# The heads of a second attention in pairs, their scores one pair ahead in alternating PSUM banks

## The chip, the core and the metric

The kernel runs on one core of one Trainium2 chip. The metric is the device time of one execution in microseconds, and the number compared is the median of several runs.

## What is computed

Two blocks follow each other on 256 tokens of width 1024, all in fp32. The first block (a stick-breaking attention, a recurrence, a feed-forward part) isn't touched. The second has two layers, and the change lies in each layer's attention:

```python
def global_attention(q, k, v):          # heads 0 to 7: 8 query heads, 2 key heads, 64 wide
    sc = einsum('bqkgd,bskd->bkgqs', qblk, k) * scale
    p = softmax(sc, axis=-1)
    return einsum('bkgqs,bskd->bqkgd', p, v)

def window_sink_attention(q, k, v, sink, slopes):   # heads 8 to 15, as many keys
    sc = einsum('bqkgd,bskd->bkgqs', qblk, kb) * scale - slope * dist   # NEG_INF outside the window
    m = maximum(sc.max(-1), sink)
    p = exp(sc - m); p = p / (p.sum(-1) + exp(sink - m))
    return einsum('bkgqs,bskd->bqkgd', p, vb)

for l in range(2):
    qa, ka, va, qb, kb, vb = split(h @ w_in[l])      # qa, ka: RMS norm and rotation
    oa, ob = rms_norm(global_attention(qa, ka, va)), rms_norm(window_sink_attention(qb, kb, vb, ...))
    h = layer_norm(ALPHA * h + concat([oa, ob]) @ w_o[l])
    h = layer_norm(ALPHA * h + peer_ffn(h))
```

## The kernel before

It is written engine by engine: `tensor`, `scalar`, `vector`, `gpsimd` and `sync` each issue their own instructions in a fixed order by hand, and semaphores tie them (`s.up(key, step)` marks a step, `w.wait_ge(*s.to(step))` waits for it). So each engine is a queue in program order: what stands behind a waiting instruction waits too. `emptied(b)` on TensorE waits until PSUM bank `b` has been read by whoever reads it last (`free[b]`). There are eight banks of 128x512 fp32.

Weights come as units of 128x1024. SyncE loads them into three raw slots, ScalarE rounds them into a high part (`hi`, L1123, two halves of 128x512 a unit), GpSimd or VectorE subtracts to get the low part (`lo`, GpSimd's at L2341). High and low parts have six halves each, so three units are ready ahead. A product takes three matmuls (high by high, high by low, low by high) in place of an fp32 one.

The attention of a layer works on 16 heads of 64 numbers. Heads 0 to 7 are the first group (global attention), 8 to 15 the second (window and sink). `QT` holds the transposed queries and keys: tiles 0 to 3 the queries of the first group, 4 its keys, 5 to 8 and 9 the same of the second. Each tile has the heads of key head 0 on partitions 0 to 63 and those of key head 1 on 64 to 127 (`PAR`), so head 0 and head 4 share tile 0 and lie on different partitions. For a head:

- TensorE `at_scores`: two fp32 matmuls of contraction 64, 256 columns each, into bank `h % 2`. An fp32 matmul stands as two records in the trace.
- VectorE `at_scores`: row maximum (L2062) and its product with the scale (L2069) for the first group; for the second, distance bias (L1621, writes `WS`), maximum, maximum with the sink, scale (L1618). It gives `nmx`.
- ScalarE `at_scores`: two exponentials with sums (L1135) into `PX[h % 3]`.
- TensorE `at_turn`: four 128x128 transposes (L445) into bank `2 + h % 2`; VectorE (heads 0 to 7, L2117) or ScalarE (8 to 15, L1514) copies the bank to `PT`.
- TensorE `at_pv`: four fp32 matmuls of 64 columns into banks 6 and 7 (first group) or 4 and 5 (second).

The loop runs over single heads, 18 steps; in step `h` TensorE issues the scores of head `h`, transposes head `h-1`, issues five filler matmuls (`warm`, bf16, into a score bank; nothing reads the result), and makes the value product of head `h-2`:

```python
        for h in range(18):
            if h < 16: at_scores(h)
            if h < 2: project(2, 2 + h, 4)
            if 5 <= h < 10: turn_tile((9, 5, 6, 7, 8)[h - 5], 2 + h % 2, ("qb", l))
            if h in (15, 16): turn_out("oa", [h - 15], OA)
            if 1 <= h <= 16:
                at_turn(h - 1)
                if h > 2: warm((h - 1) % 2, 5)
            if h == 17: out_product(0)
            if h >= 2: at_pv(h - 2)
```

`project(2, g, 4)` are the last two quarters of the input projection. `turn_tile` transposes the second group's query and key tiles, one a step from step 5 on, copied by VectorE (L2019). Inside the same loop VectorE scales the residual `H` and adds its bias (`gain_step`, L1959, four of 128x1024, steps 4 to 7), and normalises the first group's output: `over` (reciprocal of the sums), `values` (L2089), `head_mean`, `head_root`, `head_norm` (L2107), for which GpSimd squares (L2402) and ScalarE takes a root, with a table load before and after. `turned`/`turn_out` transpose the normalised output for the output product: TensorE, then ScalarE (high part), then VectorE (low part, L1621). `out_product(n)` takes the units of `w_o`, 12 matmuls of 512 columns each; 0 to 3 need the first group alone, 4 to 7 the second. After the loop come turns 2 and 3 of the first group, products 1 to 3, the second group's turns (its normalisation runs on VectorE and ScalarE meanwhile), products 4 to 7 and a layer norm.

## Time and profile before

| | us |
|---|---|
| median of 3 runs | 2468.97 |
| lowest and highest run | 2467.76, 2470.97 |
| the profiled execution's own time | 2468.69 |
| its span, first to last instruction | 2466.9 |
| TensorE, VectorE, ScalarE, GpSimd busy in it | 2406.5, 1682.1, 1261.8, 541.0 |
| head loop of layer 0, first score matmul to first output product | 58.43 |
| the same of layer 1 | 58.43 |

The profile is of one execution. Busy time of an engine is the time in which at least one of its instructions runs; matmuls overlap in it, so starts, not durations, tell how long TensorE takes for a group. The granted clock is the share of full speed at which TensorE's clock was let through.

The columns of the rows further down: in a timeline, start in us from the span's start, duration in us, engine, line, operation, written tile <- read tiles, partitions x elements, how many instructions are merged (x), and in brackets the idle time before and what ended it. In the windows view, the stretch, its length, then busy us and instructions of TensorE's matmuls (PE), its weight loads (PEld), VectorE (DVE), ScalarE (ACT) and GpSimd (POOL), then the granted clock, the DMA engines' busy share and GB/s. `arena`, `pb` and `cst` are the SBUF area of all working tiles, the PSUM banks and the constants.

### The profile page before, as it was taken

The numbers are of one execution on the slowest core, as the hardware profiler recorded it, in microseconds if no ns is written. First come the engines' busy times: TensorE is split into PE (matmuls) and PEld (weight loads), VectorE is DVE, ScalarE is ACT, GpSimd is POOL, SyncE is SP. The second block draws the span as 40 slices with busy tenths as digits, with TensorE's granted clock in tenths as the row PEclk, the third lists the DMA queues.
The fourth block names the chain that finished last, engine by engine and source line by source line (L and its number), as shares of the span: only waits on it lengthen the run. The fifth ranks groups of instructions, "written<-read, shape, count | busy, mean of one in ns | idle before, by whom it ended". The sixth has DMA issues, their size and how long they took to land.

```text
span 2466.9 us, 42599 instructions
## 1 busy us (share of the span) xinstructions
PE 2406.5 (98%) x16775; PEld 2183.0 (88%) x16775; DVE 1682.1 (68%) x3026; ACT 1261.8 (51%) x2689; POOL 541.0 (22%) x423
## 2 busy tenths in 40 slices
PE   7999999999999999999999999999999999999997
PEld 6888989998789999999888888789999999888886
DVE  4737345446669767887777556659776888777556
ACT  6542335445555544445555555545455455555554
POOL 3640224546178300000000002358500000000000
PEclk9999999999999999999999999999999999999999
DMA  5320145564145666666777665235666666787664
GB/s 179 121 87 17 36 153 169 188 188 143 49 156 171 186 181 194 195 195 193 241 245 224 195 211 151 90 113 168 183 187 185 195 193 193 227 247 237 195 199 145
DMA packets 148069, 421.00 MB, mean 171 GB/s; under 512 B 15904, under 2 KB 49056, under 8 KB 147488
## 3 DMA queue, kind: packets, MB, share of 16 engines
q1 hardware_dynamic: 144080, 405.34, 53.2%
q0 software_dynamic: 2192, 8.99, 1.0%
q10 hardware_dynamic: 1600, 3.96, 0.5%
q8 instruction: 134, 2.20, 0.4%
q14 instruction: 63, 0.52, 0.1%
HBM read 400.40 MB, written 17.83 MB: 170 GB/s over the span
## 4 chain that ended last, share of the span: by engine, by line
PE 92%; DVE 4%; ACT 2%; DMA 1%; issue 0%; POOL 0%; ACTq 0%; DVEq 0%
PE pb L436 91%; PE pb L445 1%; ACT arena L1135 1%; DVE arena L1618 1%; DVE arena L1621 0%; ACT L1135 0%; DVE arena L1767 0%; DMA raw<-in_vT 0%; DMA H<-in_x 0%; ACT hi L1123 0%; DVE H L1618 0%; DVE sm L1932 0%; DVE arena L2062 0%; DVE arena L1791 0%; DMA raw<-in_w_out 0%
## 5 line engine op out<-in xcount | busy, mean ns | idle before, releaser
L1123 ACT CAST hi<-raw 128x512 fp32r<-128x512 f32 x1402 | 819.2, 620 | 376.4 <-PE pb L436 192.5
L436 PE MATMUL pb<-HTh,hi 128*128 128x256 f32 (+1 forms) x2968 | 858.9, 289 | 2.6 <-POOL lo L2341 1.9
L436 PE MATMUL pb<-HTh,lo 128*128 128x256 f32 (+1 forms) x2968 | 842.2, 284 | 0.0
L436 PE MATMUL pb<-HTl,hi 128*128 128x256 f32 (+1 forms) x2968 | 842.2, 284 | 0.0
L2341 POOL TENSOR_TENSOR lo<-raw,hi 128x512 fp32r<-128x512 f32 x383 | 520.2, 1382 | 564.1 <-ACT hi L1123 564.1
L1628 DVE TENSOR_TENSOR lo<-raw,hi 128x1024 fp32r<-128x1024 f32 x464 | 565.3, 1218 | 85.7 <-ACT hi L1123 85.5
L436 PEld LDWEIGHTS pb<-HTh,hi 128*128 128x128 f32 x2968 | 569.7, 192 | 7.2 <-issue 2.7
L436 PEld LDWEIGHTS pb<-HTl,hi 128*128 128x128 f32 x2968 | 570.1, 192 | 0.9
L436 PEld LDWEIGHTS pb<-HTh,lo 128*128 128x128 f32 x2968 | 569.6, 192 | 0.0
L436 PE MATMUL pb<-hi,WH 128*128 128x512 f32 x1112 | 433.6, 390 | 4.3 <-DVE WL L2305 4.3
L436 PE MATMUL pb<-lo,WH 128*128 128x512 f32 x1112 | 433.2, 390 | 0.0
L436 PE MATMUL pb<-hi,WL 128*128 128x512 f32 x1112 | 433.0, 389 | 0.0
L1135 ACT ACTIVATE arena<-pb 128x256 f32<-128x256 f32 (+1 forms) x301 | 114.8, 382 | 472.8 <-PE pb L436 469.8
L2348 POOL DMA_DIRECT2D arena<-in_ln_g x4 | 2.3, 563 | 1273.9 <-PE pb L436 1273.9
L2305 DVE TENSOR_TENSOR WL<-arena,WH 128x256 fp32r<-128x256 f32 x256 | 109.9, 429 | 230.0 <-ACT WH L1587 229.0
L436 PEld LDWEIGHTS pb<-hi,WH 128*128 128x128 f32 x1112 | 208.9, 188 | 48.2 <-ACT arena L1135 3.1
L436 PEld LDWEIGHTS pb<-hi,WL 128*128 128x128 f32 x1112 | 208.8, 188 | 43.2
L436 PEld LDWEIGHTS pb<-lo,WH 128*128 128x128 f32 x1112 | 208.9, 188 | 42.5
L436 PE MATMUL pb<-arena 128*128 128x128 f32 (+13 forms) x1808 | 208.9, 278 | 4.1 <-DVE arena L1791 1.5
L436 PEld LDWEIGHTS pb<-arena 128*128 128x128 f32 (+6 forms) x1808 | 180.1, 174 | 22.1 <-issue 6.2
L1635 DVE TENSOR_TENSOR lo<-raw,hi 128x512 fp32r<-128x512 f32 x91 | 90.3, 994 | 38.7 <-ACT hi L1123 36.6
L1587 ACT CAST WH<-arena 128x256 fp32r<-128x256 f32 x256 | 102.5, 401 | 1.8 <-PE pb L436 1.8
(196 smaller groups left out, 2166.0 us busy)
## 6 DMA issues: line engine op xcount, KB each, us to landing
raw<-in_uT SPq DMA_DIRECT2D x256, 512.0 KB, 3.6
raw<-in_vT SPq DMA_DIRECT2D x256, 512.0 KB, 4.2
raw<-in_w_ffn_in SPq DMA_DIRECT2D x44, 512.0 KB, 4.0
raw<-in_wq SPq DMA_DIRECT2D x32, 512.0 KB, 3.6
wk<-kept SPq DMA_DIRECT2D x128, 128.0 KB, 3.8
raw<-in_w_in SPq DMA_DIRECT2D x24, 512.0 KB, 3.8
raw<-in_w_ffn_out SPq DMA_DIRECT2D x22, 512.0 KB, 4.4
raw<-in_w_gate SPq DMA_DIRECT2D x16, 512.0 KB, 3.3
```

What stands on the lines that cost most here:

```text
L436: return e.matmul(o, l, r, start=start, stop=stop)
L445: return e.transpose(o, i, m.C("ident")[0:n, 0:n])
L1123: e.copy(u.hi[k], u.half[k]).then_inc(*s.up("hi", ("hi", g)))
L1135: return e.activation(o, a, f, **kw)
L1587: e.copy(m.AC[j % 2][0], m.AW[:, j, :]).then_inc(*s.up("w_hi", ("w_hi", l, j)))
L1618: return e.tensor_scalar(o, a, s1, None, op0) if op1 is None else e.tensor_scalar(o, a, s1, s2, op0, op1)
L1628: x = tt(u.lo2, u.raw, u.hi2.bitcast(F32), S)
L1635: tt(u.lo[k], u.half[k], u.hi[k].bitcast(F32), S).then_inc(*s.up("lo_dve", ("lo", g)))
L2305: tt(m.AC[j % 2][1], m.AW[:, j, :], m.AC[j % 2][0].bitcast(F32), S).then_inc(*s.up("w_low", ("w_lo", l, j)))
L2341: tt(u.lo[k], u.half[k], u.hi[k].bitcast(F32), S).then_inc(*s.up("lo_pool", ("lo", g)))
L2348: e.dma_start(bc[:, 0:1024], g.partition_broadcast(128)).then_inc(*s.up(f"bc{n}", by=16))
```

## The change

On TensorE the heads are taken in eight pairs in the order 0 4, 1 5, 2 6, 3 7, 8 12, 9 13, 10 14, 11 15: one head on partitions 0 to 63 and one on 64 to 127. The matmuls of a pair's scores alternate between the two heads and between two banks, and the banks of one pair differ from those of the next (`SCORES`). The scores of pair p+1 are issued before the value products of pair p-2 and behind the transposes of pair p-1. The fillers are six before the scores of four pairs and six before the last transposes. The five tiles of the second group are transposed together in pair 2, through banks 4 and 5, and ScalarE copies them instead of VectorE. `PT` has four buffers. VectorE's residual steps go to pairs 0 (two), 2 and 4. VectorE's bias step waits for the exponential three heads before it. The first group's normalisation moves by some heads, its four turns stand behind transposes 15 and value product 14 and use banks 0 and 1, and the first output product comes behind them and behind the last value product. In the code `n` is a head's place in the new order.

```diff
+HEADS = [0, 4, 1, 5, 2, 6, 3, 7, 8, 12, 9, 13, 10, 14, 11, 15]
+TILES = (9, 5, 6, 7, 8)
+SCORES = ((0, 1), (6, 7), (0, 1), (4, 5), (0, 1), (4, 5), (0, 1), (6, 7))
...
-        self.PT = [ar(13824 + i * 512, 512) for i in range(3)]
+        self.PT = [ar(13824 + i * 512, 512) for i in range(3)] + [ar(0, 512)]
...
-FOUR, OA, OBT = (0, 1, 2, 3), (3, 2), (2, 3, 4, 5)
+FOUR, OA, OBT = (0, 1, 2, 3), (0, 1), (2, 3, 4, 5)
...
+        def at_scores(p):
+            pair = list(zip(SCORES[p], HEADS[2 * p:2 * p + 2]))
+            for b, h in pair:
+                f = 5 * (h // 8)
+                emptied(b)
+                w.wait_ge(*s.to("qt", l, f + h % 4))
+                w.wait_ge(*s.to("qt", l, f + 4))
             for t in range(2):
-                x = mm(PB[b][:, t * 256:(t + 1) * 256], m.QT[r, f + j, t * 128:(t + 1) * 128], m.QT[r, f + 4, :], True, True)
+                for b, h in pair:
+                    r, f = PAR[h % 8 // 4], 5 * (h // 8)
+                    x = mm(PB[b][:, t * 256:(t + 1) * 256], m.QT[r, f + h % 4, t * 128:(t + 1) * 128], m.QT[r, f + 4, :], True, True)
+                    if t:
+                        x.then_inc(*s.up("score_ps", ("score_ps", l, h)))
+                        free[b] = [("nmx" if h > 7 else "px", l, h)]
...
-        for h in range(18):
...
+        at_scores(0)
+        at_scores(1)
+        project(2, 2, 4)
+        project(2, 3, 4)
+        for p in range(1, 8):
+            at_turn(2 * p - 2)
+            at_turn(2 * p - 1)
+            if p < 7 and p != 2:
+                if p > 2:
+                    warm(SCORES[p + 1][0], 6)
+                at_scores(p + 1)
+            if p > 1:
+                at_pv(2 * p - 4)
+                at_pv(2 * p - 3)
+            if p == 2:
+                for k, f in enumerate(TILES):
+                    turn_tile(f, 4 + k % 2, ("qb", l))
+                at_scores(3)
+        warm(0, 6)
+        at_turn(14)
+        at_pv(12)
+        at_pv(13)
+        at_turn(15)
+        turn_out("oa", (0, 1), OA)
+        at_pv(14)
         turn_out("oa", (2, 3), OA)
+        at_pv(15)
+        out_product(0)
...
+        def weights(n):
+            w.wait_ge(*s.to("pt_ps", l, HEADS[n]))
+            w.wait_ge(*s.to("pv_ps", l, HEADS[n - 4]))
+            e.copy(m.PT[n % 4], PB[2 + n % 2][:, :]).then_inc(*s.up("soft", ("pt", l, HEADS[n])))
+
+        for p in range(8):
+            if p == 7:
                 w.wait_ge(*s.to("o_ms", l, 0))
                 fn(m.s16[:, :, 0:8], m.v16[:, :, 0:8], ACT.Sqrt).then_inc(*s.up("roots", ("o_root", l, 0)))
+            at_scores(2 * p)
+            if p == 7:
+                weights(12)
+            at_scores(2 * p + 1)
+            if p == 0:
+                take("win", l, 2, 2)
+                take("win", l, 2, 3)
+            elif p == 1:
+                second_group()
+            elif p == 2:
+                for k, f in enumerate(TILES):
+                    w.wait_ge(*s.to("qt_ps", l, f))
+                    e.copy(m.QT[:, f, :], PB[4 + k % 2][:, 0:256]).then_inc(*s.up("qkv2", ("qt", l, f)))
+            elif p == 3:
+                split_high(units.i + 3)
+            elif p == 7:
                 w.wait_ge(*s.to("sinks", l))
...
+            if 3 < p < 7:
+                weights(2 * p - 2)
+                weights(2 * p - 1)
+        weights(14)
+        turned(("oa", l), (0, 1), OA, f"gn{l}")
         turned(("oa", l), (2, 3), OA, f"gn{l}")
...
             if g:
+                w.wait_ge(*s.to("px", l, HEADS[n - 3]))
                 stt(m.WS[i], C("negd"), 8.0 * 2.0 ** -(hh + 1), src, M, A).then_inc(*up("scores"))
...
+        for p in range(8):
+            at_scores(2 * p)
+            at_scores(2 * p + 1)
+            for k in {0: (0, 1), 2: (2,), 4: (3,)}.get(p, ()):
+                gain_step(k, ("in", l), m.BC2 if l else m.bc, 2 * l)
+            if 1 <= p <= 3:
+                weights(2 * p - 2)
+                weights(2 * p - 1)
+            elif p == 5:
                 over(0)
                 values(0, 0)
                 values(0, 1)
+            elif p == 6:
                 head_mean(0, 0)
                 head_mean(0, 1)
+            elif p == 7:
+                weights(13)
                 own()
                 sink = m.bcs[:, o + 128:o + 136].unsqueeze(2).to_broadcast([128, 8, 2])
                 tt(m.snk[:, 8:16, :], m.nmx[:, 8:16, :], sink, A).then_inc(*up("scores", ("sinks", l)))
+        head_root(0)
+        head_norm(0, 0)
+        head_norm(0, 1)
+        weights(15)
+        turned(("oa", l), (0, 1, 2, 3), OA, f"gn{l}")
         over(1)
```

ScalarE's and VectorE's `at_scores` take `n` too, with `h = HEADS[n]` and the bank from `SCORES`; VectorE has a `weights(n)` of its own.

## Rows read from the trace of the kernel before

**Rows 1.** The page: busy time, share of the span and instructions of each engine.

```profile
PE 2406.5 (98%) x16775; PEld 2183.0 (88%) x16775; DVE 1682.1 (68%) x3026; ACT 1261.8 (51%) x2689; POOL 541.0 (22%) x423
```

**Rows 2.** Windows of both head loops and one spell: busy times, granted clock, DMA.

```profile
610.84:669.27 58.43, 54.27 (x356) 44.26 (x357) 40.44 (x78) 31.46 (x92) 14.20 (x13) 1.00 0.20 64
...
1550.84:1609.27 58.43, 54.27 (x352) 44.22 (x352) 40.43 (x78) 31.46 (x92) 14.23 (x13) 0.99 0.20 64
1608.30:1611.70 3.40, 3.40 (x15) 3.05 (x14) 0.91 (x3) 0.78 (x2) 0.00 (x0) 0.50 0.00 0
```

**Rows 3.** Timeline of TensorE in both loops: start us, duration, instructions.

```profile
610.84 1.13 PE L436 MATMUL pb<-arena 64*128 64x256 f32 x4 [0.52 <-DVE arena L2019]
611.89 0.51 PE L436 MATMUL pb<-hi,HTh 128*128 128x512 f32 x1
...
618.79 0.60 PE L445 MATMUL pb<-cst,arena 128*128 128x128 f32 x4
...
649.41 0.66 PE L445 MATMUL pb<-cst,arena 128*128 128x128 f32 x4
649.90 0.71 PE L436 MATMUL pb<-cst 128*128 128x256 bf16 x5
650.45 2.06 PE L436 MATMUL pb<-arena 128*128 128x64 f32 x12
652.51 0.66 PE L445 MATMUL pb<-cst,arena 128*128 128x128 f32 x4
...
666.53 0.44 PE L445 MATMUL pb<-cst,arena 128*128 128x128 f32 x2 [1.30 <-ACT arena L1514]
...
669.27 0.48 PE L436 MATMUL pb<-hi,HTh 128*128 128x512 f32 x1
...
672.11 1.00 PE L436 MATMUL pb<-arena 128*128 128x64 f32 x8
672.95 0.61 PE L445 MATMUL pb<-cst,arena 128*128 128x128 f32 x4
673.31 0.47 PE L436 MATMUL pb<-hi,HTh 128*128 128x512 f32 x1
...
681.60 1.03 PE L445 MATMUL pb<-cst,arena 128*128 128x128 f32 x8
...
1613.73 1.00 PE L436 MATMUL pb<-arena 128*128 128x64 f32 x8
```

**Rows 4.** Groups of TensorE, layer 0's loop: transposes; busy, mean, idle before, releasers.

```profile
L445 PE MATMUL pb<-cst,arena 128*128 128x128 f32 x82 | 12.8, 283 | 4.2 <-ACT arena L1135 2.4 <-ACT arena L1514 1.3 <-DVE HTl L1621 0.5
```

**Rows 5.** Timeline of TensorE, first attention: one pair of heads on different partitions.

```profile
111.49 0.70 PE L436 MATMUL pb<-arena 64*128 64x256 f32 x4 [0.47 <-ACT arena L1235]
```

**Rows 6.** Timeline of VectorE in layer 0's loop.

```profile
629.34 0.69 DVE L2062 TENSOR_REDUCE arena<-pb 128x2 f32<-128x512 f32 x1 [0.41 <-PE pb L436]
...
631.07 1.21 DVE L1959 TENSOR_TENSOR H<-H,arena 128x1024 f32<-128x1024 f32 x1
...
655.85 0.69 DVE L1621 SCALAR_TENSOR_TENSOR arena<-cst,pb 128x512 f32<-128x512 f32 x1
...
657.49 0.17 DVE L1618 TENSOR_SCALAR arena<-arena 128x2 f32<-128x2 f32 x1
```

**Rows 7.** Timeline of ScalarE in layer 0's loop.

```profile
640.93 0.51 ACT L1135 ACTIVATE arena<-arena 128x256 f32<-128x256 f32 x1 [2.97 <-DVE arena L1618]
...
641.84 0.19 ACT L1135 ACTIVATION_READ_ACCUMULATOR arena<-arena 128x1 f32 x1
...
655.39 0.56 ACT L1514 COPY arena<-pb 128x512 f32<-128x512 f32 x1
655.97 1.28 ACT L1135 ACT_TABLE_LOAD   x1
...
658.79 0.51 ACT L1135 ACTIVATE arena<-arena 128x256 f32<-128x256 f32 x1
```

**Rows 8.** Timeline of GpSimd: low parts of four halves of w_o.

```profile
675.84 5.95 POOL L2341 TENSOR_TENSOR lo<-raw,hi 128x512 fp32r<-128x512 f32 x4 [22.66 <-ACT hi L1123]
```

More of the change, by code:

```diff
@@ L949, in tensor, with at_turn @@
         turn_tile(4, 2, ("ka", l))
[L952 to L964 removed]
+        def at_scores(p):
[5 more added lines that the diff above has]
+                w.wait_ge(*s.to("qt", l, f + 4))
+            for t in range(2):
+                for b, h in pair:
[4 more added lines that the diff above has]
+                        free[b] = [("nmx" if h > 7 else "px", l, h)]
+        def at_turn(n):
+            h, i, b = HEADS[n], n % 3, 2 + n % 2
             emptied(b)
@@ L971, in at_turn, with at_pv @@
             free[b] = [("pt", l, h)]
-        def at_pv(h):
-            i, g, hh = h % 3, h // 8, h % 8
+        def at_pv(n):
+            h, i = HEADS[n], n % 4
+            g, hh = h // 8, h % 8
             vo = 768 * g + 640 + 64 * (hh // 4)
@@ L1484, in second_group, with at_scores @@
                 e.copy(m.PJ[:, t, 1408:1536], PB[4 + t][:, 384:512]).then_inc(*s.up("qkv2", ("pj", l, 2, t), *([("vb", l)] if t else [])))
-        def at_scores(h):
-            g, hh, b, i = h // 8, h % 8, h % 2, h % 3
+        def at_scores(n):
+            h = HEADS[n]
+            g, b, i = h // 8, SCORES[n // 2][n % 2], n % 3
             src = m.WS[i] if g else PB[b][:, :]
@@ L1492, in at_scores @@
                 w.wait_ge(*s.to("nmx", l, h))
[L1493 to L1494 removed]
+                if n > 2:
+                    w.wait_ge(*s.to("pt_ps", l, HEADS[n - 3]))
                 x = fn(m.PX[i][:, t * 256:(t + 1) * 256], sv[:, t, :], ACT.Exp, bias=m.nmx[:, h, t:t + 1],
@@ L1497, in at_scores @@
                 x.then_inc(*s.up("soft", *([("px", l, h)] if t else [])))
-        for h in range(18):
-            if h == 2:
-                second_group()
-            elif h == 9:
-                split_high(units.i + 3)
-            elif h == 13:
+        def weights(n):
[4 more added lines that the diff above has]
+            if p == 7:
                 w.wait_ge(*s.to("o_ms", l, 0))
                 fn(m.s16[:, :, 0:8], m.v16[:, :, 0:8], ACT.Sqrt).then_inc(*s.up("roots", ("o_root", l, 0)))
-            if h < 16:
-                at_scores(h)
-            if h < 2:
-                take("win", l, 2, 2 + h)
-            if 9 <= h <= 16:
-                w.wait_ge(*s.to("pt_ps", l, h - 1))
-                w.wait_ge(*s.to("pv_ps", l, h - 4))
-                e.copy(m.PT[(h - 1) % 3], PB[2 + (h - 1) % 2][:, :]).then_inc(*s.up("soft", ("pt", l, h - 1)))
-            if h in (15, 16):
-                turned(("oa", l), [h - 15], OA, f"gn{l}")
-            if h == 15:
+            at_scores(2 * p)
[14 more added lines that the diff above has]
+            elif p == 7:
                 w.wait_ge(*s.to("sinks", l))
                 fn(m.snk[:, 8:16, :], m.snk[:, 8:16, :], ACT.Exp).then_inc(*s.up("soft", ("snk", l)))
+            if 3 < p < 7:
[3 more added lines that the diff above has]
+        turned(("oa", l), (0, 1), OA, f"gn{l}")
         turned(("oa", l), (2, 3), OA, f"gn{l}")
@@ L2051, in vector, with at_scores @@
         ts(m.sk8, m.bcs[:, o + 128:o + 136], 8.0, None, M).then_inc(*up("scores"))
-        def at_scores(h):
-            g, hh, b, i = h // 8, h % 8, h % 2, h % 3
+        def at_scores(n):
+            h = HEADS[n]
+            g, hh, b, i = h // 8, h % 8, SCORES[n // 2][n % 2], n % 3
             src = PB[b][:, :]
@@ L2108, in head_norm, with weights @@
             x.then_inc(*up("heads", ("os", l, g, t)))
-        for h in range(18):
-            if h < 16:
-                at_scores(h)
-            if 5 <= h < 10:
-                turn_tile((9, 5, 6, 7, 8)[h - 5], 2 + h % 2)
-            if 1 <= h <= 8:
-                w.wait_ge(*s.to("pt_ps", l, h - 1))
-                e.tensor_copy(m.PT[(h - 1) % 3], PB[2 + (h - 1) % 2][:, :]).then_inc(*up("tiles", ("pt", l, h - 1)))
-            if 4 <= h <= 7:
-                gain_step(h - 4, ("in", l), m.BC2 if l else m.bc, 2 * l)
-            if h == 10:
+        def weights(n):
+            w.wait_ge(*s.to("pt_ps", l, HEADS[n]))
+            if n > 3:
+                w.wait_ge(*s.to("pv_ps", l, HEADS[n - 4]))
+            e.tensor_copy(m.PT[n % 4], PB[2 + n % 2][:, :]).then_inc(*up("tiles", ("pt", l, HEADS[n])))
+        for p in range(8):
[7 more added lines that the diff above has]
+            elif p == 5:
                 over(0)
                 values(0, 0)
-            elif h == 11:
                 values(0, 1)
-            elif h == 12:
+            elif p == 6:
                 head_mean(0, 0)
                 head_mean(0, 1)
-            elif h == 13:
-                head_root(0)
-                head_norm(0, 0)
-            elif h == 14:
-                head_norm(0, 1)
-            elif h == 15:
+            elif p == 7:
+                weights(13)
                 own()
```

31 lines of the change are left out of this document (removed).

## The prediction

> **What bounds the kernel now.** I read the page first. TensorE is busy for 98% of the span [rows 1], and there is no core but this one, so a change in one stage counts only as far as TensorE gets through that stage sooner. Next the windows view: each layer's head loop, from the first score matmul to the first output product, is 58.43 us long with TensorE busy for 54.27 of them, the same in both layers, at the full granted clock but for a spell at its lower level (0.50) at 1608.30 in layer 1 [rows 2]. Then TensorE's own timeline [rows 3]. The reader should see that a steady head is a string of work with no gap: transposes from 649.41, five filler matmuls from 649.90, then from 650.45 in one line the value products of an older head and the scores of the next, and the next transposes at 652.51; 3.10 us a head. What the 16 heads wait for in all is one row: 4.2 us before the transposes, for ScalarE's exponentials and copies and one VectorE result [rows 4]. So the loop is bound by TensorE's instruction string and only in places by the softmax chain. VectorE and ScalarE were read last, for how long that chain is [rows 6, 7].
>
> **What the scores cost, and what pairing saves.** The scores of one head (two fp32 matmuls, four records, contraction over 64 rows) take 1.05 us from their start to the next instruction (610.84 to 611.89) [rows 3]; 16 heads, 16.8 us. The change interleaves a head on partitions 0 to 63 with one on 64 to 127, in two banks. The loop of before has no such pair, but the first attention has: four records of 64x256 in 0.70 us at 111.49 [rows 5], where four in a string take 1.13 [rows 3]; the two heads' records start together. I take a pair at 1.05, eight pairs 8.4: **saved 8.4 us**. Bounds: nothing if these pairs do not overlap, 8.4 if they do; the row is of the same shape, so the upper end.
>
> The Trainium skill, "TensorEngine Tiling (Array Packing)", sections "Tiling Modes" and "PSUM Bottleneck", speaks partly against it: changing the tiling mode drains the engine, and after the tiling the emptying of PSUM may become the bottleneck. The drain is inside the measured 1.05 and now comes 8 times instead of 16; the second is what the walk below looks for.
>
> **Fillers.** Before, 14 heads carry five bf16 fillers, 70 in all, 0.55 us for five (649.90 to 650.45), 0.11 each [rows 3]. After, five blocks of six, 30. **Saved 40 x 0.11 = 4.4 us.** They are busy time that waits may take back, so the waits have to be laid out.
>
> **Waits.** Saved: all of the old 4.2 us [rows 4]. New ones come from laying out the eight pairs in program order. TensorE: a pair of transposes 0.93 (0.49 for the first head, 649.41 to 649.90, 0.44 for the second), fillers 0.66, a score pair 1.05 and 0.1 lead, two heads of value products 1.8 (0.84 for one, 672.11 to 672.95, and its lead) [rows 3]: 4.5 us a pair against 6.2 before. VectorE: a first-group head 0.9 (reduction 0.69 and a small multiply with its wait), a second-group head 1.84 (655.85 to the end of 657.49, and the wait for itself), a scale or bias of the residual 1.2 [rows 6]; emptying a bank is taken at the reduction's 0.69. ScalarE: an exponential pair of halves 1.0, a bank copy 0.56, a table load 1.28 [rows 7].
>
> - *Start.* Two score pairs, then both projections: 610.84 + 2.1 + 5.8 = 618.75, where the first transposes stood before (618.79) [rows 3]. The 16 heads' scores are a pair further by then, and VectorE has done two scale steps in time that it idled.
> - *Pair 2.* Five q/k tile turns now stand together in two banks, copied by ScalarE behind exponentials 4 and 5. Value products 0 and 1 end at 623.55; ScalarE gets to the tiles at 624.15, the last copy ends at 626.25, and the next scores want its bank: they start at 626.3. Of 2.75 us, 1.2 are turns: **wait 1.5**. Late behind it: nothing but TensorE's own string.
> - *Pairs 3 to 5.* Scores of pair 4 start at 629.05, of 5 at 633.6, of 6 at 638.2: TensorE's 4.5 a pair. The chain from a score start is 1.2 (scores done), 3.65 (two heads on VectorE), 1.0 (exponential), 0.5 (copy) = 6.4 us, and the transposes that need it stand 7.4 us behind that start: 1 us of slack, no wait.
> - *Pair 6 to 7.* VectorE waits for value product 7 (641.15) before it scales the first group's output (0.69 twice), and the reductions of pair 6, whose scores are done at 639.35, are queued behind it. Their results come at 644.5 and 646.35; ScalarE's exponential of head 13 ends at 647.4, and its copy of transpose 10, queued behind that, at 647.95. Transpose 12 writes the bank which that copy empties; TensorE has been free since 645.6: **wait 2.35**.
> - *Pair 7.* ScalarE changes its table for the root and back (2.8 us, as 655.97 to 658.79 before [rows 7]) until 651.25, exponential 14 ends at 652.25, copy 12 at 652.8; transpose 14 waits for its bank from 651.3: **wait 1.5**.
> - *End.* The last turns of the first group cost about 0.4; the output products start at 658.6, value product 15 and all turns behind them already. Before, they start at 669.27 but the product after the first only at 673.31, since the last value product and two turns stand between [rows 3]. Level with 673.31 is 658.6 + 2.75 = 661.35: 11.96 us sooner.
>
> **Sum.** By parts, 8.4 + 4.4 + 4.2 - (1.5 + 2.35 + 1.5 + 0.4 = 5.75) = 11.3 us a layer; by the layout 11.96. I take 11.7. Parts moved at no cost: PT's fourth buffer; VectorE's added wait for the exponential three heads back (done by then); the residual's four steps, 4.8 us of VectorE, of which two lie before 618.75 and two behind reductions that are early. If that cover goes, a step is 1.2. The five tile copies are 5 x 0.3 more for ScalarE, in the 1.5. No DMA is moved past another queue; SyncE and GpSimd issue as before.
>
> **Does it come through?** The second group's chain begins when value product 15 ends. Before, it fits behind three products: its turns start at 681.60, right behind the third [rows 3]. After, it has four. GpSimd makes low parts at 5.95 / 4 = 1.49 a half, 2.98 a unit [rows 8], against 2.84 of a product (669.27 to 672.11); three units are ready, so five later ones could lag by 0.7 us. That stays in the range.
>
> **Clock.** After the same waits, 1.30 us at 666.53 among them, only layer 1 got its spell at 0.50, and there value product 15 starts 62.89 us behind the first score instead of 61.27: a spell costs 1.62 us [rows 2, 3, 5]. The new waits are longer and the fillers fewer, so I expect a spell in each layer, one more than now.
>
> 2 x 11.7 - 1.6 = 21.8 us. The profiled execution took 2468.69 us, span 2466.9; span after 2445.1. The median of the runs is 0.28 above that execution: **2468.97 - 21.8 = 2447.2 us**. Its own range: no spells and no new waits but the two at the pairs 6 and 7, 2442; 3 us more of waits a layer, 2453.
>
> **Rivals.**
> 1. *The softmax chain paces the second group.* The 1 us of slack is thin, and VectorE's other work sits in the same queue. If all four pairs 4 to 7 take 6.4 instead of 4.5, that is 7.6 us less the 3.85 already counted: gain 8.0 a layer, 2454.6. For it: VectorE's load a pair is 3.7 plus extras. Against: the extras stand in two pairs alone. Chance 0.12.
> 2. *The paired scores run in a string.* 8.4 us come back, about 3 of them inside the new waits: gain 6.3 a layer, 2458. Against it stands 111.49 [rows 5]. Chance 0.03.
> 3. *It is paid back later*: the second group's chain or the low parts hold TensorE at the output products until what was won is gone: no change, 2467. What they can hold by the rows above is under 1 us. Chance 0.04.
> 4. *Slower: TensorE's clock.* With 40 fillers gone and micro-waits between groups the granted clock could stay at 0.50 (1.2 GHz). At 1.62 us a spell it takes seven spells a layer to eat 11.7 us; the whole loop at the lower level would double 41.5 us of work: 2 x (41.5 - 11.7) = 60 slower, 2529. Against: in both layers a loop with 4.2 us of waits got at most one spell. Chance 0.03.
>
> On rival 4 the Trainium skill, "TensorE: Matmul & The Clock Gate", section "A second HAM failure mode: psum-queue depth-cycling", says that short idles between groups of matmuls that cycle through PSUM banks can make the clock swing between its levels again and again. By that rule this loop, with alternating banks, would lose time as rival 4 does; by the rows of before, whose loop also cycles banks, it does not.
>
> **Chances.** The forecast 0.78. A difference under 0.2% (4.9 us) is about what a measurement of this kernel cannot tell from none. Faster: forecast, rivals 1 and 2, 0.93; within 0.2%: rival 3 and the near side of 4, 0.04; slower 0.03. Range for 8 in 10: 2439 (no waits beyond 3 us a layer, no spells) to 2457 (rival 1 with 1 us more of waits a layer).
>
> **What would show it.** TensorE's score rows come as eight records in about 1.13 us, 8 times a layer; 30 fillers a layer; the head loop's window from the first score to the first output product about 47.8 us instead of 58.43. Waits before transposes 12 and 14 on ScalarE's copies, and before the fourth score pair on ScalarE's last tile copy. The second group's turns follow the fourth product. One spell at 0.50 near the loop's end in each layer. The prediction is wrong if transposes wait in every pair, if the score pairs take 2 us, or if the stretch between the loop and the layer norm has grown.

## The result and the profile after

| | before | after |
|---|---|---|
| median of 7 runs, us | 2470.97 | 2448.77 |
| lowest and highest run | 2467.76, 2471.92 | 2440.83, 2456.60 |
| the profiled execution's own time, its span | 2468.69, 2466.9 | 2454.43, 2452.6 |
| granted clock, mean of the span | 0.993 | 0.988 |

The ratio of the times is 0.9912, 95% interval 0.9898 to 0.9927: faster by 0.9%, 22.2 us between the medians where 21.8 were predicted. The runs of after spread over 15.8 us, those of before over 4.2.

The page of after, busy times, to be held against [rows 1]: TensorE has 13.7 us less, 80 matmuls fewer, which are the fillers.

```profile
PE 2392.8 (98%) x16695; PEld 2173.9 (89%) x16695; DVE 1676.7 (68%) x3016; ACT 1264.9 (52%) x2699; POOL 541.3 (22%) x423
```

The windows of both head loops of after (first score to first output product) and of a spell in each, as in [rows 2]:

```profile
609.58:662.27 52.69, 48.76 (x329) 42.15 (x329) 39.38 (x74) 33.77 (x99) 14.43 (x13) 0.87 0.20 71
647.20:660.80 13.60, 13.43 (x65) 13.12 (x65) 7.30 (x16) 7.53 (x18) 0.00 (x0) 0.50 0.01 1
1544.94:1597.57 52.63, 48.71 (x328) 42.10 (x329) 39.39 (x74) 33.77 (x99) 14.45 (x13) 0.87 0.20 71
1582.40:1596.10 13.70, 13.37 (x65) 13.06 (x65) 7.32 (x17) 7.69 (x18) 0.00 (x0) 0.50 0.00 0
```

Layer 0's loop is 5.7 us shorter than before, not the 10.6 that were forecast (58.43 to about 47.8), and the granted clock says why: it is 0.87 in the mean, because each loop holds a spell of 13.7 us at 0.50, TensorE's lower level (1.2 GHz). TensorE was busy for 13.4 of these 13.7 us, so this is work done slowly. In layer 1 the gain is 6.7: the loop of before is 59.35 there, not 58.43, because its first output product starts only at 1610.19, behind the end of the window in [rows 2]:

```profile
1610.19 0.77 PE L436 MATMUL pb<-hi,HTh 128*128 128x512 f32 x1
```

A second profile of the same kernel (the run `after_again` below) happens to have no spell in layer 0's loop and 3.4 us of one in layer 1's:

```profile
611.15:659.42 48.27, 42.98 (x328) 35.96 (x329) 39.51 (x75) 33.58 (x99) 14.42 (x13) 1.00 0.24 77
1541.78:1590.09 48.31, 44.36 (x328) 37.66 (x329) 39.56 (x75) 33.59 (x99) 14.46 (x13) 0.96 0.23 77
```

That is the loop which the prediction laid out: 48.27 us long (47.8 predicted). TensorE's timeline of it, from the second group's tiles in pair 2 on; the rows answer to [rows 3]. The last row is ScalarE's, the copy that empties the bank of transpose 10:

```profile
624.51 0.71 PE L448 MATMUL pb<-cst,arena 128*128 128x128 f32 x4 [0.55 <-ACT arena L1541]
625.41 0.44 PE L448 MATMUL pb<-cst,arena 128*128 128x128 f32 x2 [0.19 <-ACT arena L1541]
626.30 1.13 PE L439 MATMUL pb<-arena 64*128 64x256 f32 x8 [0.46 <-ACT arena L1541]
627.37 1.09 PE L448 MATMUL pb<-cst,arena 128*128 128x128 f32 x8
...
629.05 3.06 PE L439 MATMUL pb<-arena 64*128 64x256 f32 x24
631.95 1.04 PE L448 MATMUL pb<-cst,arena 128*128 128x128 f32 x8
...
637.35 1.14 PE L448 MATMUL pb<-cst,arena 128*128 128x128 f32 x8 [0.71 <-ACT arena L1523]
...
642.27 1.14 PE L448 MATMUL pb<-cst,arena 128*128 128x128 f32 x8
...
648.92 1.14 PE L448 MATMUL pb<-cst,arena 128*128 128x128 f32 x8 [1.86 <-ACT arena L1523]
...
653.81 0.66 PE L448 MATMUL pb<-cst,arena 128*128 128x128 f32 x4 [1.35 <-ACT arena L1523]
...
641.66 0.56 ACT L1523 COPY arena<-pb 128x512 f32<-128x512 f32 x1
```

Read it in pairs of heads. The scores of a pair are eight records in 1.13 us at 626.30, and the next thing starts 1.07 later. Three waits of the prediction's layout are there: at the tiles 0.55 + 0.19 + 0.46, before transpose 12 (648.92) 1.86, before transpose 14 (653.81) 1.35. Two are there that it didn't have: 0.71 before transpose 8 (637.35), and a small one before transpose 10 (642.27), which carries no mark of its own. That transpose stands 4.92 behind transpose 8, where a pair without a wait takes 4.5, and it starts 0.05 behind the end of ScalarE's copy (641.66 + 0.56); so some 0.4 went there.

To compare loops whatever stands at their end, I take the "level": from the first score to the product behind the first output product, 62.47 us before in layer 0 (673.31 in [rows 3] less 610.84). It is 51.11 in `after_again`: **11.36 us a layer at the full clock**. With the 13.7 us spell it is 55.54: the spell costs 4.43. Layer 1 of before has a spell of its own in [rows 2], and its level is 64.09.

### The profile page after: what moved, and what is told of

The parts are those of the page before. It is cut to its first block and busy times, and to the rows that moved or that the text cites. A ratio compares the mean times of both kernels' runs of the same rounds, so it can differ in the third digit from the quotient of the medians.

```text
span 2452.6 us, 42445 instructions
## 1 busy us (share of the span) xinstructions
PE 2392.8 (98%) x16695; PEld 2173.9 (89%) x16695; DVE 1676.7 (68%) x3016; ACT 1264.9 (52%) x2699; POOL 541.3 (22%) x423
## 5 line engine op out<-in xcount | busy, mean ns | idle before, releaser
L439 PE MATMUL pb<-arena 128*128 128x128 f32 (+13 forms) x1808 | 196.2, 282 | 5.0 <-DVE arena L1823 1.5
L439 PEld LDWEIGHTS pb<-arena 128*128 128x128 f32 (+6 forms) x1808 | 174.1, 178 | 23.8 <-issue 9.8
```

The costliest lines, as they stand in the source:

```text
L439: return e.matmul(o, l, r, start=start, stop=stop)
```

## The experiments

Each time is a median; "before" is the old kernel on the same chip, and the interval is that of the ratio. The level and the spells at 0.50 inside the loops are those of each profiled execution.

| kernel | us | before | ratio, 95% | level, layers 0 and 1 | spells, layers 0 and 1 |
|---|---|---|---|---|---|
| after_again | 2449.03 | 2469.21 | 0.9905 to 0.9935 | 51.11, 51.16 | none, 3.4 |
| same_rows | 2457.63 | 2469.21 | 0.9940 to 0.9964 | 61.69, 55.84 | 3.4 + 13.7, none |
| fill_waits | 2445.55 | 2469.21 | 0.9892 to 0.9921 | 51.13, 51.39 | none |
| copies_first | 2441.79 | 2469.21 | 0.9869 to 0.9898 | 50.17, 50.19 | none |
| before_30_fill | 2481.14 | 2469.56 | 1.0025 to 1.0058 | 68.74, 69.31 | 27.3, 27.3 |
| residual_late | 2451.38 | 2469.56 | 0.9910 to 0.9937 | 52.85, 53.10 | 6.8, 6.8 |
| copies_fill | 2444.96 | 2469.56 | 0.9882 to 0.9911 | 50.17, 50.88 | none |
| root_late | 2445.12 | 2469.56 | 0.9875 to 0.9906 | 50.80, 50.77 | none |
| scores_behind | 2443.61 | 2468.02 | 0.9883 to 0.9913 | 50.29, 50.31 | none |
| no_fill | 2454.49 | 2468.02 | 0.9925 to 0.9952 | 55.81, 55.94 | 6.8 + 10.2, 10.2 + 6.8 |
| cast_late | 2441.77 | 2468.02 | 0.9879 to 0.9909 | 49.19, 50.92 | none, 6.8 |
| copies_first_2 | 2444.47 | 2468.02 | 0.9886 to 0.9916 | 50.18, 50.20 | none |

### after_again: the changed kernel once more

No edit. 

> The changed kernel once more, as the reference of the three below. Theory A (the gain is saved TensorE work, and spells at the lower clock level give some of it back, by chance more or less from run to run): the median lies between 2441 and 2457 again, runs spread by over 8 us, and a run's time rises as its mean granted clock falls. Theory B (the spread is noise of the measurement and has nothing to do with the clock): times and mean clock do not go together.

It gives 2449.03, and the loop without a spell, shown above. The runs spread over 10.2 us, and longer runs have the lower clock in the main: over the 7 runs of after and these 6, a straight line through time and clock gives 0.35 us for each us at 0.50. Theory A stands, though not run by run (2451.83 came at 0.988, 2453.98 at 0.990).

### same_rows: what the two halves of the array are worth

```diff
-HEADS = [0, 4, 1, 5, 2, 6, 3, 7, 8, 12, 9, 13, 10, 14, 11, 15]
+HEADS = [0, 1, 2, 3, 4, 5, 6, 7, 8, 9, 10, 11, 12, 13, 14, 15]
```

The order of the work stays, but both heads of a pair lie on the same partitions. 

> The pairs are 0 1, 2 3, 4 5 and so on, both heads of a pair on the same partitions, all else as in the changed kernel. Theory A (8.4 us a layer come from two heads' score matmuls running at once): a pair's eight records take 2.1 us instead of 1.14; TensorE's string is 8.4 us a layer longer, of which waits swallow up to 3: 11 to 17 us slower than the changed kernel, 2460 to 2466. Theory B (the gain comes from the fillers and the waits alone, the scores are hidden): within 3 us of the changed kernel.

TensorE's timeline of it: a pair alone, and a string of a pair and two value products (3.06 us at 629.05 above).

```profile
627.64 1.99 PE L439 MATMUL pb<-arena 64*128 64x256 f32 x8 [0.46 <-ACT arena L1541]
...
643.63 3.92 PE L439 MATMUL pb<-arena 64*128 64x256 f32 x24
```

A pair takes 1.99 in place of 1.13, 0.86 more, 6.9 a layer. The level of layer 1, which has no spell here, is 4.7 longer, because waits give back most of the rest: those before transposes 8 and 10 are gone (1.1), the one before transpose 12 is 1.32 instead of 1.86, the first one at the tiles 0.24 instead of 0.55. The medians differ by 8.6 us, under the 11 to 17 that I expected. So overlap is real, and it is the largest part of the gain, but only two thirds of it come through.

### before_30_fill: the fillers alone

The kernel before, with 30 fillers a layer instead of 70 and nothing else changed:

```diff
-                    warm((h - 1) % 2, 5)
+                    warm((h - 1) % 2, 3 if h in (15, 16) else 2)
```

> The kernel before with 30 fillers a layer in its head loop in place of 70 (two a head, three in two heads), all else as before. Theory A (the fillers are part of TensorE's string, 0.11 us each, where it has no wait): each loop is up to 4.4 us shorter at full clock, less what the waits of the second half take back; with one more short spell at the lower clock level: 3 to 8 us faster than the kernel before. Theory B (the loop of before is bound by the softmax chain, fillers only fill): no change within 2 us. Theory C (the fillers held the clock up): spells of several windows a layer, slower than before.

It is slower than before by 11.6 us: theory C. The windows view of layer 0's loop and of the spell in each layer:

```profile
610.44:675.15 64.71, 62.37 (x316) 49.79 (x317) 40.72 (x77) 31.43 (x92) 14.18 (x13) 0.79 0.16 58
645.90:673.20 27.30, 27.30 (x101) 21.52 (x99) 13.33 (x31) 12.50 (x35) 2.08 (x2) 0.50 0.03 10
...
1594.80:1622.10 27.30, 27.30 (x103) 21.78 (x100) 13.62 (x33) 11.59 (x33) 2.08 (x2) 0.50 0.05 19
```

With 40 matmuls fewer the loop is 6.28 us longer than [rows 2] (64.71 against 58.43), since 27.3 us of it ran at the lower level. TensorE's timeline on both sides of the fall:

```profile
644.78 0.63 PE L445 MATMUL pb<-cst,arena 128*128 128x128 f32 x4 [1.54 <-ACT arena L1135]
...
648.76 1.11 PE L445 MATMUL pb<-cst,arena 128*128 128x128 f32 x4
...
653.83 1.12 PE L445 MATMUL pb<-cst,arena 128*128 128x128 f32 x4
```

Up to 644.78 the edit does what was meant: that row stands 34.34 us behind the first score, where its counterpart in the kernel before (646.41, with a wait of 0.86) stands 35.57 behind it. By then 21 fillers are missing, 2.3 us, and 1.23 us have come through; longer waits took the rest back (2.14 us up to here instead of 1.10). The last of them has grown to 1.54 and the clock falls 1.1 us behind it; then a step of one head takes 5.07 (648.76 to 653.83) instead of 3.10. No gap in the loop is longer than that 1.54. What the removal would give behind that row at the full clock, no run shows.

### no_fill and fill_waits: fewer and more fillers in the changed kernel

`no_fill` takes out the 30 that are left, `fill_waits` adds 26 where TensorE waits anyway:

```diff
         for p in range(1, 8):
+            if p == 7:
+                warm(0, 16)
...
-        warm(0, 6)
+        warm(0, 16)
         at_turn(14)
```

> The changed kernel with none of its 30 fillers a layer. At full clock 3.3 us of string less a layer, of which waits take back what is in front of them. Theory A (what a filler buys is the granted clock: without them the loop runs at the lower level for much of its length, as the kernel before did for 27 us with 30 instead of 70): spells of 14 us or more in both loops, 0 to 12 us slower than the changed kernel. Theory B (fillers are only work): 3 to 6 us faster.

> The changed kernel with 16 more fillers before transpose 12 and 16 instead of 6 before transpose 14, where TensorE waits for 1.9 and (at full clock) 1.5 us. Theory A (the long spell at 0.50 near each loop's end comes of TensorE's idle time there and costs 4 to 5 us a layer): the spell goes, runs draw together, 6 to 9 us faster than the changed kernel, 2440 to 2443. Theory B (fillers are only work; the spell comes of something else, as the slow exchange of heads itself): no gain, same spells, 0 to 3 us slower.

`no_fill`: the two spells in layer 0's loop, windows view.

```profile
639.90:646.70 6.80, 6.80 (x34) 5.70 (x30) 3.51 (x8) 3.13 (x10) 0.85 (x1) 0.50 0.00 0
653.50:663.70 10.20, 9.16 (x45) 8.97 (x44) 5.46 (x12) 5.71 (x16) 0.00 (x0) 0.50 0.01 2
```

`fill_waits`: TensorE's timeline from transpose 12 on.

```profile
645.43 1.91 PE L439 MATMUL pb<-cst 128*128 128x256 bf16 x16
...
650.16 1.91 PE L439 MATMUL pb<-cst 128*128 128x256 bf16 x16
652.34 0.66 PE L448 MATMUL pb<-cst,arena 128*128 128x128 f32 x4 [0.27 <-ACT arena L1525]
```

Without fillers the wait before transpose 8 grows to 2.03, the loop holds 17.0 us at 0.50, and the time is 2454.49: 30 fillers (3.3 us) a layer less to do, and 5.5 us longer in all than `after_again`. That comparison is across two chips and the intervals overlap a little (up to 0.9935, from 0.9925); the three other kernels run beside `no_fill` on its chip are 10 to 13 us faster, with intervals apart. With 26 more layer 0's loop is as long as in `after_again` (48.29 against 48.27), as a filler in a wait costs nothing; layer 1's is 0.2 longer, for a longer wait at the tiles. Neither loop has a spell. The median, 2445.55, is 3.5 us under `after_again`, not the 6 to 9 of theory A, and the intervals overlap, so that the fillers keep the spells away is suggested and not shown; the highest of its 4 runs is 2447.52, of 6 runs of `after_again` 2453.98.

### copies_first: which wait holds transpose 12

ScalarE copies the transposed weights 10 and 11 ahead of exponentials 12 and 13, not behind them.

```diff
+            if p == 6:
+                weights(10)
+                weights(11)
             at_scores(2 * p)
...
-            if 3 < p < 7:
+            if 3 < p < 6:
                 weights(2 * p - 2)
```

> The changed kernel, but in pair 6 ScalarE copies transposes 10 and 11 before its exponentials 12 and 13, not behind them. Theory A (transpose 12 waits 1.9 us for a bank that a copy empties, and the copy waits in ScalarE's queue behind an exponential whose maximum is late on VectorE): transpose 12 starts with exponential 12, transpose 13 waits under 1 us, the loop is 1.0 to 1.3 us shorter a layer: 2 to 3 us faster at the same clock. Theory B (the late maximum itself holds TensorE): the wait moves whole to transpose 13 and nothing is gained.

> copies_first again, beside the three others. If its gain over the changed kernel was more than chance, the median is 2438 to 2445 and no loop has a spell longer than one of 3.4 us; else it falls among the changed kernel's 2441 to 2457.

TensorE's waits in the second half of its loop:

```profile
635.91 1.14 PE L448 MATMUL pb<-cst,arena 128*128 128x128 f32 x8 [0.71 <-ACT arena L1523]
647.01 0.66 PE L448 MATMUL pb<-cst,arena 128*128 128x128 f32 x4 [0.95 <-ACT arena L1154]
651.41 0.66 PE L448 MATMUL pb<-cst,arena 128*128 128x128 f32 x4 [1.36 <-ACT arena L1523]
```

Transpose 12 no longer waits; transpose 13 does, 0.95 for its own exponential. The loop gets 0.95 shorter, in both layers and in both profiles of this kernel: theory A. The first time the median was 7.2 us under `after_again` on the same chip, with intervals apart. 1.9 us of that are the waits; the rest may be spells that don't come (granted clocks 0.993 to 0.996, against 0.988 to 0.993). The second time, on another chip, it was 2444.47: inside the range expected, with no spell in a loop, but 23.6 us under the kernel before instead of 27.4, and its interval overlaps those of `after_again` and of after. The 0.95 a layer is shown, the 7 us is not.

`copies_fill` is this with 8 and 16 fillers ahead of transposes 12 and 14.

> ScalarE's copies of transposes 10 and 11 first, as in copies_first, and fillers in the waits that are left: 8 before transpose 12, 16 instead of 6 before transpose 14. Theory A (fillers in a wait cost nothing and keep the clock up): loops as long as those of copies_first at full clock, no spell in them, a median 0 to 3 us below that of copies_first, 2439 to 2442, and a spread under 5 us. Theory B (the fillers delay the transposes they stand before): 1 to 3 us slower than copies_first.

The loop is that of `copies_first` in layer 0 and 0.7 longer in layer 1, half of it in a wait of 0.92 instead of 0.58 at the tiles. 2444.96 where 2439 to 2442 were expected: nothing more is won by it.

### root_late: the table load and the root behind exponential 15

On top of `copies_fill` ScalarE takes the root after the last copy, and the four turns of the first group stand together behind value product 15. VectorE copies transpose 15 before it finishes the norm. The fillers differ too: 12 instead of 16 before transpose 14, and six new ones before the turns.

> As copies_fill, and ScalarE takes the first group's root, with its two table loads, behind exponentials 14 and 15 and copy 14 instead of ahead of them; the group's four turns stand behind value product 15 and use four banks. Theory A (the 2.8 us of table loads in front of exponential 14 are what holds transpose 14): its wait falls by 1 to 1.5 us, but the root and the norms come later and the first output product waits for them up to 2 us: loop 1 us shorter to 1 us longer. The second group's chain starts about 1.5 us sooner, which helps nothing while four products cover it. 2438 to 2443. Theory B (transpose 14 waits for VectorE's maximum): no difference there, and 1 to 2 us a layer slower at the end.

TensorE at transpose 14, and ScalarE's exponential 14:

```profile
653.23 1.47 PE L439 MATMUL pb<-cst 128*128 128x256 bf16 x12
654.76 0.66 PE L448 MATMUL pb<-cst,arena 128*128 128x128 f32 x4
...
653.14 0.51 ACT L1156 ACTIVATE arena<-arena 128x256 f32<-128x256 f32 x1 [2.19 <-DVE arena L1653]
```

No wait is marked before transpose 14, because the 12 fillers cover it. From the value products' end it takes 1.53 us to the transpose (653.23 to 654.76) instead of the 2.17 of `copies_fill`: the table loads held it for 0.6 us, not for 1 to 1.5, and behind them stands VectorE's maximum, for which ScalarE now waits (2.19). At the end the turns start only when VectorE's norm is done, the six fillers cover that, and 0.52 stands at the first output product (DVE's low part); the turns have lost their cover. The level is 0.63 longer than that of `copies_fill` in layer 0, the time the same (2445.12). The 1.35 us of transpose 14 can be moved in part, but aren't won this way.

### residual_late: VectorE's residual steps in pairs 3 to 6

```diff
-            for k in {0: (0, 1), 2: (2,), 4: (3,)}.get(p, ()):
+            for k in {3: (0,), 4: (1,), 5: (2,), 6: (3,)}.get(p, ()):
```

> The changed kernel with the residual's four steps on VectorE one each in pairs 3, 4, 5 and 6 instead of two in pair 0 and one each in 2 and 4. Theory A (VectorE's queue is what holds transposes 12 and 14, so a 1.2 us step ahead of them counts in full): the waits before transposes 12 or 14 grow by 1 to 2.4 us together, the loops get longer by as much: 2 to 5 us slower than the changed kernel. Theory B (VectorE has room in every pair): within 1 us.

2451.38. The waits grow in other places than theory A had them: before transpose 12 there are still 1.86 and 1.83, but before transpose 8 the wait is 0.92 instead of 0.71, and in layer 1 transpose 10 waits 0.49. Both loops have a spell of 6.8. How much of the 1.7 to 1.9 us of level belongs to the waits and how much to the clock, these runs don't separate, and the interval overlaps that of `after_again`.

### scores_behind: must the scores stand ahead of the value products?

```diff
-                at_scores(p + 1)
             if p > 1:
                 at_pv(2 * p - 4)
                 at_pv(2 * p - 3)
+            if p < 7 and p != 2:
+                at_scores(p + 1)
```

This starts a pair's scores two value products, some 1.8 us, later in TensorE's order. 

> The changed kernel, but a pair's scores are issued behind the two value products instead of ahead of them, 1.8 us later in TensorE's string; no instruction more or less. Theory A (scores issued early are what keeps the chain of scores, maximum, exponential and copy under TensorE's string, with about 1 us to spare in a pair): transposes wait about 1 us in each pair from 4 on and 1.8 more before 12: loops 3 to 6 us longer, 6 to 12 us slower in all than the changed kernel. Theory B (the place does not matter, TensorE's work decides): within 2 us.

I expected it to be slower. TensorE's timeline:

```profile
627.19 1.09 PE L448 MATMUL pb<-cst,arena 128*128 128x128 f32 x8
...
631.67 1.09 PE L448 MATMUL pb<-cst,arena 128*128 128x128 f32 x8
...
637.38 1.14 PE L448 MATMUL pb<-cst,arena 128*128 128x128 f32 x8 [1.17 <-ACT arena L1524]
...
642.31 1.14 PE L448 MATMUL pb<-cst,arena 128*128 128x128 f32 x8 [0.33 <-ACT arena L1524]
...
647.91 1.14 PE L448 MATMUL pb<-cst,arena 128*128 128x128 f32 x8 [1.01 <-ACT arena L1524]
...
652.80 0.66 PE L448 MATMUL pb<-cst,arena 128*128 128x128 f32 x4 [1.36 <-ACT arena L1524]
```

The waits come earlier, 1.17 and 0.33, and the one before transpose 12 shrinks from 1.86 to 1.01. The four add up to 3.87; in `after_again` the three are 3.92, and 4.3 with the unmarked one. So the chain of the softmax costs no more with the scores in the later place: the waits change places. A pair without a wait is 0.1 shorter besides (627.19 to 631.67, 4.48, against 627.37 to 631.95, 4.58), and the level is 0.82 less. Theory A fell. The median is 5.4 under `after_again`, on another chip and with intervals that overlap.

### cast_late: who makes transpose 8 wait

`copies_first`, and `split_high(units.i + 3)` with GpSimd's `split_low` moved behind weights 14 and behind the squares, so that GpSimd makes no low part at pair 3:

```diff
-            elif p == 3:
-                split_high(units.i + 3)
...
         weights(14)
+        split_high(units.i + 3)
         turned(("oa", l), (0, 1), OA, f"gn{l}")
...
-        split_low(units.i + 3)
...
+        split_low(units.i + 3)
         for n in range(8):
```

> As copies_first, and ScalarE's rounding of the third output unit (and with it GpSimd's two low parts of it) comes behind copy 14 instead of in pair 3. Theory A (the 0.7 us wait before transpose 8 comes of VectorE's small multiply of the pair before, 1.20 us long in place of 0.17 while GpSimd makes a low part): that multiply falls to 0.2, the wait before transpose 8 goes, the loop is 0.7 us shorter than that of copies_first (47.3), 46.6. Theory B (VectorE's load of two heads and a residual step is the cause): no difference. The unit's low part is ready 3 us before its product at worst, nothing lost there.

In `after_again` VectorE's last two small operations on head 8 (128 x 2 numbers each) run into GpSimd's low part; VectorE's timeline, then GpSimd's, then ScalarE's exponential 8:

```profile
631.37 0.69 DVE L2096 TENSOR_REDUCE arena<-arena 128x2 f32<-128x512 f32 x1
632.09 0.48 DVE L2099 TENSOR_TENSOR arena<-arena 128x2 f32<-128x2 f32 x1
632.60 1.20 DVE L1650 TENSOR_SCALAR arena<-arena 128x2 f32<-128x2 f32 x1
...
635.34 0.16 DVE L2099 TENSOR_TENSOR arena<-arena 128x2 f32<-128x2 f32 x1
635.53 0.17 DVE L1650 TENSOR_SCALAR arena<-arena 128x2 f32<-128x2 f32 x1
```

```profile
631.27 1.27 POOL L2377 TENSOR_TENSOR lo<-raw,hi 128x512 fp32r<-128x512 f32 x1 [8.40 <-ACT hi L1142]
632.51 1.26 POOL L2377 TENSOR_TENSOR lo<-raw,hi 128x512 fp32r<-128x512 f32 x1
...
633.83 0.51 ACT L1154 ACTIVATE arena<-arena 128x256 f32<-128x256 f32 x1 [2.12 <-DVE arena L1650]
```

And in `cast_late`, the same operation of VectorE, and TensorE at transposes 8, 10 and 13:

```profile
632.04 0.17 DVE L1652 TENSOR_SCALAR arena<-arena 128x2 f32<-128x2 f32 x1
```

```profile
636.23 1.04 PE L448 MATMUL pb<-cst,arena 128*128 128x128 f32 x8
...
640.75 1.07 PE L448 MATMUL pb<-cst,arena 128*128 128x128 f32 x8
...
647.24 0.66 PE L448 MATMUL pb<-cst,arena 128*128 128x128 f32 x4 [1.12 <-ACT arena L1154]
```

The operation takes 0.17 instead of 1.20, neither transpose 8 nor transpose 10 waits, and pairs follow each other at 4.52 us (636.23 to 640.75), the 4.5 of the prediction. 0.17 of it come back before transpose 13. The edit also takes ScalarE's rounding out of pair 3, but that wasn't what held the pair: in `after_again` ScalarE had stood idle for 2.12 us when VectorE's operation let it go. Layer 0's loop is the shortest of all, 46.35, 0.97 less than in `copies_first`. Layer 1 got a spell of 6.8 again and stayed at 48.07, so that the median, 2441.77, isn't told apart from `copies_first_2` on the same chip.

## Why the prediction was right

- **Paired scores, 8.4 a layer: right in size.** A pair costs 1.07 to the next instruction (1.05 taken). By `same_rows` 6.9 of the 8.4 are overlap; the other 1.5 come from eight groups in place of sixteen, as a pair on the same partitions takes 1.92 to the next instruction and two single heads 2.1. Taken alone the overlap is worth 4.7, because part of the new waits vanishes with a slower string; the prediction counted those waits as a term of their own.
- **Waits: the three named ones right in place, near in size.** Tiles 1.2 (1.5), transpose 12 1.86 (2.35), transpose 14 1.35 (1.5). With the two below they are 5.5 where the prediction had 5.35 ahead of the loop's end.
- **"Pairs 3 to 5: 1 us of slack, no wait": failed.** Waits of 0.71 and some 0.4 stood there. From the start of the scores to the copy that frees the bank of transpose 8 it took 8.2 us (629.05 to 637.29), not 6.4. About 0.4 of that is VectorE's copies of transposes 4 and 5, which stand ahead of head 8 in its queue. 1.35 is VectorE's two small operations, 1.20 instead of 0.17 and 0.48 instead of 0.16 because GpSimd was at a low part, which I had not laid beside them. `cast_late` shows it by taking that work away: 6.9 us, and no wait.
- **Sum, 11.3 by parts and 11.96 by layout, 11.7 taken: 11.36 measured** at the full clock, in layer 0. The two unforeseen waits (1.1) and the 0.9 by which the other three were taken too long nearly cancel, so the sum is nearer than its parts; the rest of the layout's 0.6 is in small steps (a product takes 2.84, not 2.75).
- **The fillers' term: fits at the full clock, wrong as a price.** The 4.4 us were not measured by themselves in the changed kernel; they fit into its sum. In `before_30_fill` TensorE's time is saved less what waits take back, 1.23 of 2.3 us up to the fall of the clock. But `before_30_fill` has this term alone, and it is 11.6 us slower, not 8.8 faster. In the whole change it doesn't show so badly: its spells are 3.4 to 13.7 us long in the three profiled loops that have one, not 27.3.
- **The clock's term: right in kind, mis-sized.** One spell more, costing 1.62, was counted. The profiled execution of after has 13.7 us in both loops, 4.43 in layer 0; that of `after_again` has none in one loop and 3.4 in the other. Two levels at 11.36 would give 22.7 us; those of the profiled execution of after give 15.5 (6.93, and 64.09 - 55.48 = 8.61), and the whole execution is 14.3 faster than before's. The 1.3 between lie outside the loops and no run explains them; in `fill_waits` such a remainder is 2.6 the other way. The spread of the runs goes with the clock: their granted clocks go from 0.987 (2456.60) to 0.996 (2440.83). 0.009 of 2450 us is 22 us of clock, that is 44 us more at 0.50, for 15.8 us of time: 0.36 us lost for each us of a spell, near the 4.43 / 13.7 = 0.32 of the loop. That the median came out at the forecast (a gain of 22.2 for 21.8) is partly luck: with 1.6 us for the clock the forecast matches the median of seven runs, whose gains lie between 14.4 and 30.1, and not the profiled one.
- **The rivals.** Rival 1 did not decide but was at work in a small way: each of the transposes 8, 10, 12 and 14 waited, yet the waits beyond those counted came to 1.1 us, not to 3.75, and without GpSimd's low part they are gone. Rival 2 is refuted by 1.13 us for eight records. Rival 3 is refuted by the rows below (no change would have been 2469, not the 2467 written there). Rival 4 did not decide, but its mechanism, time lost to the clock with 40 fillers gone, is the one at work in what the terms above leave: `before_30_fill` has it without the rest of the change.
- **The prediction read 58.43 us for both loops; layer 1's is 59.35.** Its price of a spell, 1.62, was taken from other rows and agrees with the levels (64.09 - 62.47).

For rival 3, TensorE's timeline at the second group's turns and the product behind them, two rows of after and one of before:

```profile
673.28 1.03 PE L448 MATMUL pb<-cst,arena 128*128 128x128 f32 x8
674.84 0.47 PE L439 MATMUL pb<-hi,HTh 128*128 128x512 f32 x1 [0.52 <-DVE HTl L1653]
...
683.15 0.47 PE L436 MATMUL pb<-hi,HTh 128*128 128x512 f32 x1 [0.52 <-DVE HTl L1621]
```

The turns start right behind the fourth product, with no wait, and the product behind them waits 0.52 as it did before: nothing of what the loop won is paid back there.

What stays open is why one execution of the same kernel gets a spell and the next doesn't, and whether the three small gains (copies ahead, scores behind, low part late) add up: they were not put into one kernel. Each alone, `copies_first`, `scores_behind` and `cast_late` at 2441.8 to 2444.5, is faster than the kernel before, and under the changed kernel in the median. But the intervals of the three runs on the second chip overlap those of the changed kernel, which wasn't run there, and none of them is told from another.

## What to carry to other kernels

Small matmuls of contraction 64 are worth pairing on the two halves of the partitions, in two banks: price it as half of their time, then subtract what the chain behind them will take back as waits, here a third. Filler matmuls in a loop with waits are not free time to collect: take them out only together with the waits, put them where TensorE waits anyway (26 of them cost nothing in `fill_waits`), and test their removal by itself. When a profile shows a new wait of under 1 us, look at what the other engines do in the instruction that is late, not only at the order of the queues.

## What the hardware showed that I had not expected

- **The clock fell without any long gap.** The waits before the transposes of layer 0 in `before_30_fill` are 0.26, 0.34, 1.54 and 0.20, 2.3 us in all against 4.2 before [rows 4] (the last one behind the fall), and yet it ran 27.3 us at 0.50, busy for all of them. What stood ahead of the fall was the 1.54 and 2 fillers a head in place of 5. The Trainium skill, "TensorE: Matmul & The Clock Gate", section "A second HAM failure mode: psum-queue depth-cycling", has short idles between groups of matmuls swing the clock. These runs agree so far: both loops of `before_30_fill` and of `no_fill` got spells, no loop of `fill_waits` did. But with the same 30 fillers `after_again` had none in one loop and the profile of after 13.7 us in the same place, so the number of fillers alone doesn't decide.
- **The price of a spell depends on what lies behind it.** 0.32 and 0.36 us are lost for each us of a spell in the changed kernel. In `before_30_fill` the level is (68.74 - 62.47) / 27.3 = 0.23 longer for each us, but that is net of the fillers it has less, so it isn't a price. A spell of 3.4 in layer 1's loop of `after_again` cost 0.05: it starts just behind the start of transpose 12 (1579.57) and TensorE is busy all through it, but the wait of 1.35 before transpose 14 is gone, so the lower clock only filled a wait.
- **VectorE's tiniest operations stop for GpSimd.** At 632.09 a 128 x 2 operation took 0.48 instead of 0.16 and the next 1.20 instead of 0.17. GpSimd's two subtractions end at 632.54 and 633.77; VectorE's two end at 632.57 and 633.80. Not every VectorE operation stops: the reduction at 631.37 lay over the first subtraction and took its usual 0.69. The Trainium skill, "SBUF — State Buffer", section "SBUF: two separate sides", says that VectorE and GpSimd share a pair of ports, which one of them holds for a whole instruction while the other, if it needs them, stands still. The trace agrees: both ends fall 0.03 us behind an end of GpSimd's.
